# Delta rule of a two-block transformer kernel on one core: inverse in 32-wide diagonal tiles, state update in 64x64 quadrants

## The reference, cut to what matters

```python
    k_beta = k * beta[..., None]
    a_mat = jnp.einsum("bhnid,bhnjd->bhnij", k_beta, k) * decay_strict
    eye = jnp.eye(CHUNK, dtype=jnp.float32)
    t_inv = lax.linalg.triangular_solve(eye + a_mat, jnp.broadcast_to(eye, a_mat.shape),
                                        left_side=True, lower=True)
    u = t_inv @ (v * beta[..., None])
    w = t_inv @ (k_beta * jnp.exp(g)[..., None])
    p = jnp.einsum("bhnid,bhnjd->bhnij", q, k) * decay_causal
...
    def step(state, xs):
        q_c, k_c, u_c, w_c, p_c, gl = xs
        v_new = u_c - jnp.einsum("bhcd,bhde->bhce", w_c, state)
        o = (jnp.einsum("bhcd,bhde->bhce", q_c, state)
             + jnp.einsum("bhij,bhje->bhie", p_c, v_new))
        state = state * jnp.exp(gl)[..., None, None] + jnp.einsum("bhcd,bhce->bhde", k_c, v_new)
        return state, o
```

## Time and profile before

| | |
|---|---|
| median of 3 executions | 2782.16 us (2778.82 to 2782.26) |
| the profiled execution | 2778.42 us, its span 2776.6 us |
| busy over the span | PE 95%, DVE 68%, ACT 45%, Pool 15% |
| mean granted TensorE clock | 0.985 |
| the chain of work that ended last | PE 78%, DVE 11%, ACT 4%, Pool 3% |
| the delta rule | about 466 to 628 us of the span |

### The profile page before, as it was taken

How to read it: one execution, slowest core, us unless ns; L and a number is a source line. 1 busy time by engine, 2 the same in 40 slices (tenths; PEclk the granted TensorE clock), 3 DMA queues, 4 the chain that set the end, 5 groups by cost and what they waited for, 6 DMA issues and landing times.

```text
span 2776.6 us, 39285 instructions
## 1 busy us (share of the span) xinstructions
PE 2643.3 (95%) x15530; PEld 2137.2 (77%) x15530; DVE 1879.3 (68%) x2265; ACT 1237.7 (45%) x2316; POOL 408.6 (15%) x354
## 2 busy tenths in 40 slices
PE   7999998999799999999999999899998999999997
PEld 6887566887688888888778888655677888888886
DVE  3466554664687777888974664489646655578889
ACT  3323565332777773333553333467316433343332
POOL 4322001347300000000300000001375000000002
PEclk9999999999999999999999999999999999999999
DMA  3210000004356664332323123411253232343333
GB/s 135 54 38 15 8 6 25 3 21 171 106 168 211 189 198 164 117 121 107 137 91 121 62 91 106 168 60 35 89 196 112 101 111 103 122 164 109 121 106 122
DMA packets 213489, 290.49 MB, mean 105 GB/s; under 512 B 16552, under 2 KB 143807, under 8 KB 213311
## 3 DMA queue, kind: packets, MB, share of 16 engines
q1 hardware_dynamic: 195918, 227.75, 24.8%
q10 hardware_dynamic: 17392, 60.30, 5.5%
HBM read 220.91 MB, written 67.11 MB: 104 GB/s over the span
## 4 chain that ended last, share of the span: by engine, by line
PE 78%; DVE 11%; ACT 4%; POOL 3%; issue 3%; DMA 1%; SPq 0%; ACTq 0%; DVEq 0%; POOLq 0%
PE ps L1739 7%; PE ps L1741 7%; PE ps L1740 7%; PE ps L1794 6%; PE ps L1796 6%; PE ps L1795 6%; PE ps L1877 4%; PE ps L1879 4%; PE ps L1878 4%; PE ps L1530 3%; PE ps L1436 2%; PE ps L1309 1%; PE ps L1311 1%; PE ps L1310 1%; PE ps L1676 1%
## 5 line engine op out<-in xcount | busy, mean ns | idle before, releaser
L1794 PE MATMUL ps<-down_t_hi,down_s_hi 128*128 128x512 f32 x896 | 349.4, 390 | 4.0 <-DVE acc L3332 2.2
L1796 PE MATMUL ps<-down_t_hi,down_s_lo 128*128 128x512 f32 x896 | 348.7, 389 | 0.0
L1795 PE MATMUL ps<-down_t_lo,down_s_hi 128*128 128x512 f32 x896 | 348.6, 389 | 0.0
L2492 ACT CAST down_s_hi<-down_a 128x2048 fp32r<-128x2048 f32 x56 | 107.2, 1915 | 368.7 <-PE ps L1796 327.1
L1142 POOL TENSOR_SCALAR mean_sq<-ssq 128x1 f32<-128x1 f32 x64 | 36.6, 571 | 1294.7 <-ACT squares_junk_ffn L2030 1244.6
L1739 PE MATMUL ps<-act_hi,up_hi 128*128 128x512 f32 (+1 forms) x544 | 205.7, 378 | 6.1 <-issue 2.8
L1740 PE MATMUL ps<-act_lo,up_hi 128*128 128x512 f32 (+1 forms) x544 | 204.9, 377 | 0.0
L1741 PE MATMUL ps<-act_hi,up_lo 128*128 128x512 f32 (+1 forms) x544 | 204.8, 376 | 0.0
L1794 PEld LDWEIGHTS ps<-down_t_hi,down_s_hi 128*128 128x128 f32 x896 | 168.2, 188 | 41.7 <-issue 7.4
L1796 PEld LDWEIGHTS ps<-down_t_hi,down_s_lo 128*128 128x128 f32 x896 | 168.2, 188 | 35.3
L1795 PEld LDWEIGHTS ps<-down_t_lo,down_s_hi 128*128 128x128 f32 x896 | 168.2, 188 | 34.6
(11 more groups left out here) (383 smaller groups left out, 6511.6 us busy)
## 6 DMA issues: line engine op xcount, KB each, us to landing
down_a<-hid_spill SPq DMA_DIRECT2D x32, 1024.0 KB, 6.6
hid_spill<-up_hid ACTq DMA_DIRECT2D x30, 1024.0 KB, 6.2
w_ada<-in_w_ada SPq DMA_DIRECT2D x48, 512.0 KB, 4.0
up_raw<-in_w_in SPq DMA_DIRECT2D x18, 1024.0 KB, 5.1
raw<-in_w_out SPq DMA_DIRECT2D x32, 512.0 KB, 3.7
up_raw<-in_w_up SPq DMA_DIRECT2D x16, 1024.0 KB, 5.6
down_b<-in_w_down SPq DMA_DIRECT2D x16, 1024.0 KB, 6.5
up_raw<-in_w_mlp_in SPq DMA_DIRECT2D x16, 1024.0 KB, 5.3
```

Source lines behind the costliest of these rows:

```text
L1794: pe.matmul(out, ops["s_hi"][:, k, cols], ops["t_hi"][:, k, :], start=first, stop=False, skip_group_check=True)
L1795: pe.matmul(out, ops["s_hi"][:, k, cols], ops["t_lo"][:, k, :], start=False, stop=False, skip_group_check=True)
L1796: mm = pe.matmul(out, ops["s_lo"][:, k, cols], ops["t_hi"][:, k, :], start=False, stop=last, skip_group_check=True)
```

## The change

The constants hold 32-wide masks. The inverse of the diagonal is now held in 32-wide tiles: a tile of the 16 diagonal 32x32 systems is 128 x 128 floats, 4 blocks side by side on each of 4 groups of 32 partitions. Levels 1 to 4 work on these with `diagonal_products` (16 matmuls, 32 records). Level 5 is the corner: `corner_products` (8 matmuls, 16 records) from 32 partitions each. `gdn_system` has four operations of half width where it had two, and before level 5 the vector engine places the 32-wide inverses in a 64-wide tile `t_inv_T_all`. `gdn_state_update` splits each of its four products in two by output rows, in an order that goes over all four quadrants. `gdn_prepare` moves from levels 1 and 3, after the state update, to levels 2 and 4, ahead of the state products. Pool makes the masks for level 5 no more and waits for `tr0_done` in place of `a_t_done`. ACT and Pool keep their order.

```diff
+    for n, s in enumerate(LEVELS[:-1]):
+        c[:, C_LEVEL + n * SUB:C_LEVEL + (n + 1) * SUB] = ((k[:, :SUB] // s) % 2 == 1) & (r % SUB // s == k[:, :SUB] // s - 1)
+    c[:, C_FIRST], c[:, C_SECOND] = r[:, 0] // SUB % 2 == 0, r[:, 0] // SUB % 2 == 1
+    c[:, C_FIRST_NEG] = -c[:, C_FIRST]
...
             def gdn_levels(i, n):
                 for a in range(2):
                     if i or n >= 3:
                         pool.wait_ge(sem("y_prod"), 10 * i + (2 * (n - 3) + a + 1))
-                    pool.wait_ge(sem("a_t_done"), 2 * i + a + 1)
-                    pool.tensor_tensor(m_s[(n + i) % 2][a][:], a_t[i % 2][a][:], each_block(C_LEVEL + n * CHUNK), ALU.mult)\
+                    pool.wait_ge(sem("tr0_done"), 2 * i + a + 1)
+                    pool.tensor_tensor(m_s[(n + i) % 2][a][:], a_d[i % 2][a][:], each_diagonal(C_LEVEL + n * SUB), ALU.mult)\
                         .then_inc(sem("level_done"), 1)
...
-                    if n >= 2:
+                    if 2 <= n < 4:
                         gdn_levels(i, n + 1)
...
+            def diagonal_products(bank, lhs, rhs, signal):
+
+                for n in range(GDN_BLOCKS):
+                    for q in range(P // SUB):
+                        rows = slice(q * SUB, (q + 1) * SUB)
+                        mm = pe.matmul(ps[rows, bank, n * SUB:(n + 1) * SUB], lhs(rows, n), rhs(rows, n), start=True, stop=True)
+                mm.then_inc(sem(signal), 1)
+
+            def corner_products(bank, lhs, rhs, second, signal):
+
+                for n in range(GDN_BLOCKS):
+                    for g in range(2):
+                        rows = slice(g * CHUNK + second * SUB, g * CHUNK + (second + 1) * SUB)
+                        mm = pe.matmul(ps[gdn_half(g), bank, n * SUB:(n + 1) * SUB], lhs(rows, n), rhs(rows, n), start=True, stop=True)
+                mm.then_inc(sem(signal), 1)
...
-                        for g in range(2):
-                            mm = pe.matmul(ps[:, 5 + g, h * P:(h + 1) * P], k_d[a][gdn_half(g), 2 * h + c, :],
+                        for g, m in ((0, 0), (1, 1), (0, 1), (1, 0)):
+                            mm = pe.matmul(ps[gdn_half(m), 5 + g, h * P:(h + 1) * P], k_d[a][gdn_half(g), 2 * h + c, gdn_half(m)],
                                            v_n[gdn_half(g), h, :], start=True, stop=True)
...
+                    if more and n in (2, 4):
+                        gdn_prepare(i + 1, n // 2 - 1)
                     if i and not last:
                         gdn_state_products(i - 1, n - 1)
                     for a in range(2):
-                        pe.wait_ge(sem("level_done"), 10 * i + (2 * (n - 1) + a + 1))
+                        if not last:
+                            pe.wait_ge(sem("level_done"), 8 * i + (2 * (n - 1) + a + 1))
...
-                        block_products(a, lambda h, c, rows, b: m_s[(n + i) % 2][a][rows, b, :],
-                                       lambda h, c, rows, b: t_f[f_old][a][rows, b, :], CHUNK, "y_prod")
+                        if last:
+                            corner_products(a, lambda rows, b: a_t[i % 2][a][rows, b, :], lambda rows, b: t_f[f_old][a][rows, b, :], 0, "y_prod")
+                        else:
+                            diagonal_products(a, lambda rows, b: m_s[(n + i) % 2][a][rows, b, :],
+                                              lambda rows, b: t_f[f_old][a][rows, b, :], "y_prod")
                     if i and not last:
                         gdn_state_update(i - 1, n - 1)
-                    if more and n in (1, 3):
-                        gdn_prepare(i + 1, n // 2)
-                    elif last:
+                    if last:
                         gdn_turns(i, 0)
                     for a in range(2):
                         pe.wait_ge(sem("y_done"), 10 * i + (2 * (n - 1) + a + 1))
-                        block_products(a, lambda h, c, rows, b: y_s[a][rows, b, :],
-                                       lambda h, c, rows, b: t_r[old][a][rows, b, :], CHUNK, "zt_prod")
-                        if not last:
-                            block_products(2 + a, lambda h, c, rows, b: t_r[old][a][rows, b, :],
-                                           lambda h, c, rows, b: y_s[a][rows, b, :], CHUNK, "z_prod")
+                        if last:
+                            corner_products(a, lambda rows, b: y_s[a][rows, b:b + 2, :].rearrange("p b t -> p (b t)"),
+                                            lambda rows, b: t_r[old][a][rows, b, :], 1, "zt_prod")
+                        else:
+                            diagonal_products(a, lambda rows, b: y_s[a][rows, b, :], lambda rows, b: t_r[old][a][rows, b, :], "zt_prod")
+                            diagonal_products(2 + a, lambda rows, b: t_r[old][a][rows, b, :], lambda rows, b: y_s[a][rows, b, :], "z_prod")
...
-                ch.link(dve.tensor_tensor(tr[:], at[:], each_block(C_LEVEL), ALU.mult))
-                dve.tensor_tensor(tr[:], each_block(C_ID64), tr[:], ALU.subtract).then_inc(sem("tr0_done"), 1)
+                ch.link(dve.tensor_scalar(ad[:], at[:, :, SUB:CHUNK], row_half(C_SECOND), None, ALU.mult))
+                ch.link(dve.scalar_tensor_tensor(ad[:], at[:, :, 0:SUB], row_half(C_FIRST), ad[:], ALU.mult, ALU.add))
+                ch.link(dve.tensor_tensor(tr[:], ad[:], each_diagonal(C_LEVEL), ALU.mult))
+                dve.tensor_tensor(tr[:], each_diagonal(C_ID32), tr[:], ALU.subtract).then_inc(sem("tr0_done"), 1)
...
                     if last:
+                        for a in range(2):
+                            dve.wait_ge(sem("t_done"), 8 * i + 6 + a + 1)
+                            dve.tensor_scalar(t_all[a][:, :, 0:SUB], t_r[old][a][:], row_half(C_FIRST), None, ALU.mult)
+                            ch.link(dve.tensor_scalar(t_all[a][:, :, SUB:CHUNK], t_r[old][a][:], row_half(C_SECOND), None, ALU.mult))
                         gdn_scaled(i, 0)
                     for a in range(2):
                         dve.wait_ge(sem("zt_prod"), 10 * i + (2 * (n - 1) + a + 1))
-                        ins = dve.tensor_tensor(t_r[new][a][:], t_r[old][a][:], block_bank(a), ALU.subtract)
                         if last:
-                            ins.then_inc(sem("t_last_done"), 1)
+                            dve.scalar_tensor_tensor(t_all[a][:, :, SUB:CHUNK], diagonal_bank(a), row_half(C_FIRST_NEG),
+                                                     t_all[a][:, :, SUB:CHUNK], ALU.mult, ALU.add).then_inc(sem("t_last_done"), 1)
```

More of the change, by code:

```diff
@@ L354 @@
 C_LEVEL = 640
-C_ID64 = C_LEVEL + CHUNK * len(LEVELS)
-C_CSUM64 = C_ID64 + CHUNK
+SUB = 32
+C_ID32 = 1024
+C_CSUM64 = C_ID32 + CHUNK
 C_KEYCAP = C_CSUM64 + CHUNK
@@ L361 @@
 C_QUARTER_ANGLE = C_QUARTER + 1
-N_CONST = C_QUARTER_ANGLE + 1
+C_FIRST, C_SECOND, C_FIRST_NEG = [C_QUARTER_ANGLE + 1 + n for n in range(3)]
+N_CONST = C_FIRST_NEG + 1
 V_MIXPRE, V_FFNPRE, V_QN, V_KVN, V_CONV = 0, 8, 16, 18, 19
@@ L616, in two_blocks, with diagonals @@
             ("k_w", 25), ("v_b", 29), ("u", 41), ("w_T", 45), ("k_dec", 49), ("o_inter", 53)))
-        e_d, a_t, m_s, t_f = ([blocks(f"{n}{x}_", kb + 2 * x) for x in range(2)]
-                              for n, kb in (("decay", 89), ("a_T", 93), ("a_level", 97), ("t_inv", 101)))
-        t_r = [blocks(f"t_inv_T{x}_", 105 + 2 * x) for x in range(3)]
-        y_s, p_t = blocks("level_y", 111), blocks("p_T", 113)
+        def diagonals(name, kb):
+            return [sb(f"{name}{a}", kb + a / 2, [P, GDN_BLOCKS, SUB]) for a in range(2)]
+        e_d, a_t = ([blocks(f"{n}{x}_", kb + 2 * x) for x in range(2)] for n, kb in (("decay", 89), ("a_T", 93)))
+        a_d, m_s, t_f = ([diagonals(f"{n}{x}_", kb + x) for x in range(2)] for n, kb in (("a_diag", 97), ("a_level", 99), ("t_inv", 101)))
+        t_r = [diagonals(f"t_inv_T{x}_", 103 + x) for x in range(3)]
+        y_s = [sb(f"level_y{a}", 106 + 0.75 * a, [P, GDN_BLOCKS + 1, SUB]) for a in range(2)]
+        t_all, p_t = blocks("t_inv_T_all", 108), blocks("p_T", 113)
         def t_home(i):
@@ L2252, in gdn_first @@
                 act.wait_ge(sem("t0_turned"), 2 * i + a + 1)
-                act.copy(t_f[i % 2][a][:], block_bank(2 + a)).then_inc(sem("t0_done"), 1)
+                act.copy(t_f[i % 2][a][:], diagonal_bank(2 + a)).then_inc(sem("t0_done"), 1)
             def gdn_pair(i):
@@ L3064, in gdn_pair @@
                 gdn_scaled(i, 1)
+            for a in range(2):
+                dve.memset(y_s[a][:, GDN_BLOCKS:, :], 0.0)
             dve.memset(state[0][:], 0.0).then_inc(sem("state_done"), 1)
```

31 lines of the change are left out of this document (20 added, 11 removed).

## The result

| | before | after |
|---|---|---|
| median | 2782.26 us (2778.82 to 2784.03, 5 runs) | 2802.81 us (2797.83 to 2806.37, 5 runs) |
| ratio, 95% interval | | 1.0075 (1.0064 to 1.0086) |
| profiled execution, span | 2778.42, 2776.6 us | 2804.12, 2802.3 us |
| mean granted TensorE clock | 0.985 | 0.979 |
| the stage: first sums of the preparation to the state products of the last chunk | 466.71 to 626.85: 160.1 us | 468.61 to 650.79: 182.2 us |

The account below looks back on a forecast made before the run. TensorE, 95% busy, was taken to set the pace, the state chain only 0.2 us shorter. Pairs 1 and 2 -5.0, pair 3 -1.9, pair 0 -0.7, closing steps -0.3: -7.9 us, 2774.2 against 2782.2, range 2765 to 2786.

Parts of the forecast that it names:

- Sum by steps, pairs 1 and 2: Delta rule, middle tile pairs: TensorE work and waits added step by step; -2.5 us a pair, -5.0 together, near 34.7 each.
- closing condition: Prediction's last sentence: wrong in kind if the delta-rule stage gains over 12 us or the time rises.
- Part 1: Level products 64 to 32 wide: 0.47 to 0.31 us each, ends 0.27 and 0.93; 0.95 us gained per middle step.
- Rival B: Small level products gain nothing beyond two abreast, 0.55 us each: +6 us over the pairs, 2788; chance 0.10.
- Part 2: Copies and subtractions halve: ACT's copy 0.37 to about 0.27 us, the vector engine's subtraction 0.42 to about 0.29.
- Part 3: State update in four quadrants: 0.44 us where the group takes 0.65; gain 0.2, loss 0.2 at the other end.
- Part 4: Preparation, 1.05 us of TensorE, moved ahead of state products in steps 2 and 4, covering the wait for the new state.
- pair 0: First tile pair, no state work: no gain in steps 1 to 4, level 5 and turns give 0.7 us; near 28.7.
- Rival C: TensorE takes at most one record each 29 ns, whatever its size: 32-wide products +0.46 us, total +40, 2822; chance 0.09.
- Rival E: TensorE's clock falls to 1.2 GHz after waiting for pair 0's first inverses: +60 us if held four pairs; chance 0.04.
- Rival D: Vector engine and ACT take TensorE's gain through moved decay, system and inverse-placing operations: -3 us, 2779; chance 0.13.
- slower: Whole kernel measurably slower than before, by over 0.2% (5.6 us): half of Rival B, plus Rival C and Rival E; chance 0.16.

Follow-up runs that it names:

- merged32: The changed kernel with each 32x32 product covering two neighbouring blocks' columns with the first's weights, halving those products' instructions (second block wrong): 2770.8 us, ratio 0.9953.
- stream: Not the kernel: TensorE alone issues long runs of 32x32-tile products, then 64x64 ones; 28 to 29 ns a record on 32x32 tiles, 29.3 on 64x64.
- dve_turn: The changed kernel with the transposed product of levels 2 to 16 replaced by a vector-engine transposition of the new inverse: 2776.8 us, 0.9987 of the kernel before.
- stream2: TensorE alone: bursts with rests, 64x64 tiles, then 32x32 tiles with added waits; 223 records unbroken after 19 us rest, 114 a piece with waits.

## Why the prediction was wrong

**What failed.** Not a duration. The failed step is the one that turns durations into a pair: "Sum by steps, pairs 1 and 2 (TensorE, from one state product to the next)". It lets a step cost what its records cost in the array plus what is waited for by semaphore, and has no term for the arrival of the instructions. A step of 232 to 256 records is 1.8 to 2.0 packets, at 3.7 us a packet 6.7 to 7.4 us; the three steps after 514.25 took 5.56 (two packets can be stored ahead of it), 7.24 and 7.56. In before, the same sum needs 3.7 and 4.4 us for steps of 5.45 and 6.65: hidden, but by a third only. My own closing condition ("I am wrong in kind if ... the time rises") is met.

**Point by point.**

- Part 1, a product in 0.31 us: right, 0.27; the lower end, with the ends 0.55 and 0.93 excluded. Rival B falls with it. No collision in the shared bank shows either: the trace, with 8.4 ns a record, does not agree with the Trainium skill, TensorEngine Tiling (Array Packing), Gotcha 1: PSUM Pressure, for blocks in different partitions of a bank.
- Part 2: ACT's copy 264 ns (0.27 forecast), the subtraction 286 (0.29): right.
- Part 3: the update 0.46 us (516.16 to 516.62) where 0.44 was forecast. Its worth was under-sized: 0.35 us a step, where I had a gain of 0.2 and a loss of 0.2 at the other end; measured alone it is 3.9 us in all.
- Part 4: moving the preparation was to give most of the 1.2 us in steps 1 and 3; alone it gives nothing over the whole kernel, since pair 0 loses what pairs 1 and 2 gain. I had put pair 0 at no gain and no loss from it.
- Steps: the step with the least of a stall (0.23 us) took 5.56 us, 5.45 forecast. With half the instructions (merged32) the array-and-chain sum comes out: 34.1 and 32.3 us a pair against 34.7 forecast, and 2770.8 us in all, 9.6 below the kernel before on the same chip, where I had 8. So the sum described a machine with free instructions.
- Rival C is what happened in effect, at another place and size: I had TensorE taking "no more than one record each 29 ns, whatever its size" and argued against it that 29 ns "is just what two quadrants of 58 ns give". Both are true. Two quadrants of 64x64 take 29 ns a record, and instructions arrive each 29 ns on average; the row could not tell one from the other. But the limit is on the average over a packet, not on a pair of records: a burst goes at 8.4 ns, steps whose other work is long enough lose nothing, and the other steps of pairs 1 and 2 lie 1.2 to 2.1 us above their forecasts, where C would put them 3.7 above (0.46 and 0.16 for each of six products), so +21 and not +40 us. The floor of about 25 ns from start to start that the Trainium skill gives (TensorE: Matmul & The Clock Gate, Back-to-back issue gap) does not hold over tiles that do not overlap: the records of after start 8.4 ns apart.
- Rival E (clock) had the right sign, and its place is pair 0, which I had put at 28.7 us and which takes 38.1. PE is granted 0.61 from 474 to 504 us where before had 0.95. It is not the cause of the stalls, which come at a granted clock of 1.00 in stream and in the step of 7.24 us. That the stalls lowered it is not shown either: stream stays at 1.00 with PE half idle, while dve_turn, with one such wait of 1.4 us in pair 0, is granted 0.60, and merged32, with none, 0.83. From the first sums to the first state product after takes 8.4 us longer than before, and its waits for "issue" there are 6.8 us; dve_turn, with fewer products at the same low clock, takes 3.2 longer. How many of the 22 us are the clock's stays open.
- Rival D falls: PE's idle time before level products is put down to issue, not to the vector engine. The chance that I gave for slower, 0.16, was also below its own parts, which add up to 0.18.

**What the trace of before would have said.** The queue named "instruction" has 121 packets for 2 x 15530 records: a packet is 128 records. Its packets lie 4 to 9 slices of 1.1 us apart in a stage at 128 to 152 records a step, and weight loads already wait 23 times up to 0.6 us for "issue". A change that adds 1784 records had to be held against that line: 9.9 packets a pair (1264 records) in a forecast 34.7 us leaves 3.5 us a packet, closer than any two in that stretch of before, and as little as the shortest intervals of stream. That leaves no room for a part of the pair in which the array sets the pace.

## What to carry to other kernels

Count TensorE's instructions, not only their array time: 128 float32 records (64 matmuls as written) arrive in about 3.7 us here, and no more than two such packets are stored, so a stage of small tiles must average 29 ns or more a record over a step. Splitting a product into smaller tiles pays only while the count stays under that; a product that shares its weights with its neighbour, or one that another engine can derive (a transposition of 128x128 floats in 32x32 blocks took 0.29 us), is worth more than a smaller tile. A reason of "issue" in the waits and the line of the instruction queue are the two rows to read before a change that adds instructions.

## What was not expected of the hardware

The packets' interval is 3.45 to 4.0 us with TensorE alone at work, and the same in the stage (after's stalled pieces at 529.53, 533.08 and 536.66 us lie 3.55 and 3.58 apart). Only behind the many waits of stream2, at the low clock, was it longer. Nothing that ran tells what sets it. 32x32 products run at 8.4 ns a record in the stage and at about 13.6 ns in stream (1.93 us less some 0.19 for the last record, over 128), whose weights and columns are the same bytes; why they differ was not tried. And 64x64 weights with 32 columns cost at least what 64 columns cost.
